# Two stacked blocks on one core: the operands of the split products moved to one address residue in SBUF

## What is computed

```python
for i in range(DEPTH):                       # first block, DEPTH = 2
    h = h + 0.5 * swiglu(rmsnorm(h, ffn1_norm[i]), ffn1_w_gu[i], ffn1_w_down[i])   # 1024 -> 2816 -> 1024
    u = rmsnorm(h, mix_norm[i])
    b_g, c_g, v_c, q_c, kv_c, k_r, g_conv, g_mla = jnp.split(u @ w_in[i], split_pts, axis=-1)
    y_conv = short_conv_branch(b_g, c_g, v_c, conv_w[i], w_conv_out[i])
    y_mla = mla_branch(q_c, kv_c, k_r, ...)  # latent attention, 8 heads
    h = h + (sigmoid(g_conv) * y_conv + sigmoid(g_mla) * y_mla) @ w_o[i]
    h = h + 0.5 * swiglu(rmsnorm(h, ffn2_norm[i]), ffn2_w_gu[i], ffn2_w_down[i])
    h = h + sigmoid(rmsnorm(h, ple_norm[i]) @ w_ple_gate[i]) * (p[i] @ w_ple_proj[i])
...
for i in range(DEPTH):                       # second block
    u = rmsnorm(h, norm_mix_pre[i]) @ w_in[i]
    # sparse attention over the 64 best keys, a 31-tap convolution, pooling
    h = h + rmsnorm(concat(y_attn, y_conv, y_pool) @ w_out[i], norm_mix_post[i])
    m = square(relu(rmsnorm(h, norm_mlp_pre[i]) @ w_up[i])) @ w_down[i]            # 1024 -> 4096 -> 1024
    h = h + rmsnorm(m, norm_mlp_post[i])
    h = h + sigmoid(h @ ple_gate[i]) * (p[i] @ ple_proj[i])
```

## Time and profile before

| | before |
|---|---|
| three runs, median (lowest, highest) | 1911.18 us (1909.38, 1911.8) |
| span of the profiled execution | 1909.4 us |
| TensorE busy | 1871.4 us, 98% |
| VectorE / ScalarE / GpSimd busy | 1343.1 / 998.8 / 133.0 us |
| chain that ended last | TensorE 84%, VectorE 10%, ScalarE 4% |

### The profile page before, as it was taken

How to read it: one execution, slowest core, us unless ns; L and a number is a source line. 1 busy time by engine, 2 the same in 40 slices (tenths; PEclk the granted TensorE clock), 3 DMA queues, 4 the chain that set the end, 5 groups by cost and what they waited for, 6 DMA issues and landing times.

```text
span 1909.4 us, 36805 instructions
## 1 busy us (share of the span) xinstructions
PE 1871.4 (98%) x16004; PEld 1854.5 (97%) x16004; DVE 1343.1 (70%) x1652; ACT 998.8 (52%) x1243; POOL 133.0 (7%) x110
## 2 busy tenths in 40 slices
PE   8999999999999999999999999999999999899999
PEld 8999999999999999999999999998999999899998
DVE  7755787785558655787776556888865589777655
ACT  6443545564437544545565445767534367654443
POOL 1000000000000000000000000264000006600000
PEclk9999999999999999999999999999999999899999
DMA  8655554465555555535545555423566544237651
GB/s 266 207 189 189 165 171 149 159 210 189 188 192 173 204 199 199 186 119 187 179 155 199 199 199 169 155 89 113 180 200 199 183 139 135 72 114 240 199 193 51
DMA packets 246532, 329.56 MB, mean 173 GB/s; under 512 B 6246, under 2 KB 218788, under 8 KB 246372
## 3 DMA queue, kind: packets, MB, share of 16 engines
q1 hardware_dynamic: 246018, 326.79, 51.9%
q0 software_dynamic: 96, 0.26, 0.1%
q10 hardware_dynamic: 258, 0.16, 0.0%
HBM read 326.14 MB, written 1.05 MB: 171 GB/s over the span
## 4 chain that ended last, share of the span: by engine, by line
PE 84%; DVE 10%; ACT 4%; issue 1%; DMA 1%; ACTq 0%; DVEq 0%; SPq 0%
PE work L2061 19%; PE work L2063 19%; PE work L2062 19%; PE acc L2061 9%; PE acc L2063 8%; PE acc L2062 8%; DVE w_lo L1334 3%; ACT w_hi L795 2%; DVE ra L1347 1%; DVE fa L1784 1%; PE work L2208 1%; DMA raw<-in_w_in_dram 1%; PE acc L2130 1%; DVE fa L1860 0%; DVE fa L1386 0%
## 5 line engine op out<-in xcount | busy, mean ns | idle before, releaser
L1334 DVE TENSOR_TENSOR w_lo<-raw,w_hi 128x2048 fp32r<-128x2048 f32 (+2 forms) x313 | 697.4, 2229 | 109.9 <-ACT w_hi L795 108.0
L2061 PE MATMUL work<-x_rows,w_hi 128*128 128x256 f32 x2560 | 712.3, 278 | 8.0 <-DVE w_lo L1334 4.9
L2062 PE MATMUL work<-x_rows,w_hi 128*128 128x256 f32 x2560 | 707.9, 277 | 0.0
L2063 PE MATMUL work<-x_rows,w_lo 128*128 128x256 f32 x2560 | 707.7, 276 | 0.0
L795 ACT ACTIVATE w_hi<-raw 128x2048 fp32r<-128x2048 f32 (+2 forms) x313 | 578.4, 1854 | 150.6 <-PE work L2063 67.2
L2061 PEld LDWEIGHTS work<-x_rows,w_hi 128*128 128x128 f32 x2560 | 483.8, 189 | 11.3 <-issue 6.2
L2062 PEld LDWEIGHTS work<-x_rows,w_hi 128*128 128x128 f32 x2560 | 483.8, 189 | 0.3
L2063 PEld LDWEIGHTS work<-x_rows,w_lo 128*128 128x128 f32 x2560 | 483.8, 189 | 0.0
L2061 PE MATMUL acc<-ra,w_hi 128*128 128x256 f32 x1352 | 372.4, 275 | 0.0
L2063 PE MATMUL acc<-ra,w_lo 128*128 128x256 f32 x1352 | 372.0, 275 | 0.0
L2062 PE MATMUL acc<-ra,w_hi 128*128 128x256 f32 x1352 | 372.0, 275 | 0.0
(11 more groups left out here) (318 smaller groups left out, 2267.9 us busy)
## 6 DMA issues: line engine op xcount, KB each, us to landing
raw<-in_ffn_w_gu_dram SPq DMA_DIRECT2D x88, 1024.0 KB, 5.1
raw<-in_w_in_dram SPq DMA_DIRECT2D x52, 1024.0 KB, 5.4
raw<-in_ffn_w_down_dram SPq DMA_DIRECT2D x44, 1024.0 KB, 5.0
raw<-in_w_up_dram SPq DMA_DIRECT2D x32, 1024.0 KB, 5.4
raw<-in_w_down_dram SPq DMA_DIRECT2D x32, 1024.0 KB, 4.9
raw<-in_w_mla_out_dram SPq DMA_DIRECT2D x8, 1024.0 KB, 5.5
raw<-in_w_o_dram SPq DMA_DIRECT2D x8, 1024.0 KB, 5.0
raw<-in_w_ple_gate_dram SPq DMA_DIRECT2D x8, 1024.0 KB, 5.0
```

The costliest lines, as they stand in the source:

```text
L1334: v.tensor_tensor(w_lo[:, s, 0:n], raw[:, r, 0:n], w_hi[:, s, 0:n].bitcast(F32), ALU.subtract).then_inc(lo_done.sem, 1)
L2061: pe.matmul(dst, ah, bh, start=start and i == 0, stop=False, skip_group_check=not group)
L2062: pe.matmul(dst, ah, bl, start=False, stop=False, skip_group_check=not group)
L2063: last = pe.matmul(dst, al, bh, start=False, stop=stop and i == len(pairs) - 1, skip_group_check=not group)
```

## The change

The tensors in float32r get a common helper and a common start. `rounded(name, n)` reserves 4 elements (16 bytes) more than asked and returns the tensor behind them. `w_hi` and `w_lo` become the two halves of one tensor `w`. `ra` is made longer, and `ka` and `kb` (now one tensor `keys`, the two interleaved row by row), `vp`, `rot_r` and `zero_r` become parts of it behind the old arena. `x_rows` starts its rows 4 elements in instead of 28. The other tensors are put in another order, and 64 bytes (`apart`) are left between `cols` and `x_rows`. The two memsets of `ka` and `kb` become one of `keys`.

The addresses in the built programs, bytes in a partition, and what they leave modulo 256:

| tile | before | modulo 256 | after | modulo 256 |
|---|---|---|---|---|
| `raw` | 1152 | 128 | 1152 | 128 |
| `w_hi` | 25728 | 128 | 32240 | 240 |
| `w_lo` | 58496 | 128 | 65008 | 240 |
| `xh` (in `x_rows`) | 99568 | 240 | 190192 | 240 |
| `ra` | 188144 | 240 | 128752 | 240 |
| `ka`, `kb` | 137856, 144000 | 128 | in `ra` | 240 |
| `vp` | 150144 | 128 | in `ra` | 240 |
| `rot_r`, `zero_r` | 122144, 123168 | 32 | in `ra` | 240 |
| `fa` | 157312 | 128 | 97920 | 128 |
| `h` | 91264 | 128 | 206592 | 0 |
| `consts` | 115968 | 0 | 26048 | 192 |

No instruction of TensorE or SyncE is added, removed or moved. On ScalarE and VectorE four instructions each write `ka` or `kb` in two pieces instead of one. GpSimd has one memset less.

```diff
-X_SIZE, X_ROW, X_AT = 4124, 256, (28, 2076)
+X_ROW, X_AT = 256, (0, 2048)
...
-RA_AT = 4
+R_AT = 4
+RA_SIZE = 10240
+KEYS = 2 * 3 * 2 * T
+VALUES = 2 * TB * 2 * 192
...
+        def rounded(name, n):
+
+            return sb(name, [P, R_AT + n], F32R)[:, R_AT:R_AT + n]
+
         raw = sb("raw", [P, RAWS, CH])
-        w_hi = sb("w_hi", [P, RING, CH], F32R)
-        w_lo = sb("w_lo", [P, RING, CH], F32R)
+        small = sb("small", [P, 80])
+        consts = sb("consts", [P, C_KEPT])
+        w = rounded("w", 2 * RING * CH).rearrange("p (a s n) -> p a s n", a=2, s=RING)
+        w_hi, w_lo = w[:, 0, :, :], w[:, 1, :, :]
+        joint = sb("joint", [P, 28])
+        fa = sb("fa", [P, 7704])
+        rounded_rows = rounded("ra", RA_SIZE + KEYS + VALUES + 3 * P)
+        ra, at = rounded_rows[:, 0:RA_SIZE], RA_SIZE
+        keys = rounded_rows[:, at:at + KEYS].rearrange("p (a t o n) -> p a t o n", a=2, t=3, o=2)
+        ka, kb = (keys[:, :, :, i, :] for i in range(2))
+        at += KEYS
+        vp = rounded_rows[:, at:at + VALUES].rearrange("p (a t g n) -> p a t g n", a=2, t=TB, g=2)
+        at += VALUES
+        rot_r = rounded_rows[:, at:at + 2 * P].rearrange("p (a n) -> p a n", a=2)
+        zero_r = rounded_rows[:, at + 2 * P:at + 3 * P]
+        cols = sb("cols", [P, 100])
+        sb("apart", [P, 16])
+        x_rows = rounded("x_rows", 2 * KD * T)
         h = sb("h", [P, KD, T])
-        x_rows = sb("x_rows", [P, X_SIZE], F32R)
...
-            gp.memset(ka[:, :, :, :].bitcast(F32), 0.0)
-            gp.memset(kb[:, :, :, :].bitcast(F32), 0.0)
+            gp.memset(keys.bitcast(F32), 0.0)
```

More of the change, by code:

```diff
@@ L310, in semaphore @@
             return ctx.enter_context(nc.semaphore(name))
+        def rounded(name, n):
+            return sb(name, [P, R_AT + n], F32R)[:, R_AT:R_AT + n]
         raw = sb("raw", [P, RAWS, CH])
-        w_hi = sb("w_hi", [P, RING, CH], F32R)
-        w_lo = sb("w_lo", [P, RING, CH], F32R)
+        small = sb("small", [P, 80])
[16 more added lines that the diff above has]
+        x_rows = rounded("x_rows", 2 * KD * T)
         h = sb("h", [P, KD, T])
-        x_rows = sb("x_rows", [P, X_SIZE], F32R)
-        consts = sb("consts", [P, C_KEPT])
-        rot_r = sb("rot_r", [P, 2, P], F32R)
-        zero_r = sb("zero_r", [P, P], F32R)
         vrow = sb("vrow", [P, 2, P])
@@ L326, in build @@
         rstd = sb("rstd", [P, 2, T])
[L327 to L332, removed]
         pw = sb("pw", [P, 2, P])
-        fa = sb("fa", [P, 7704])
-        ra = sb("ra", [P, RA_AT + 10240], F32R)[:, RA_AT:RA_AT + 10240]
         def cut(arena, at, *dims):
```

## The result

The changed kernel takes **1967.14 us** (median of four runs, 1958.28 to 1969.83); the kernel before, on the same chip, 1911.20 (four runs, 1909.38 to 1911.80). The ratio is 1.0287, 95% interval 1.0272 to 1.0302: slower by 55 us by the ratio, 56 by the medians. The forecast was 1993 with a range of 1904 to 2012. The profiled execution took 1958.28 us, the fastest of the four, with a span of 1956.5: 47.1 us more than the span before.

The account below looks back on a forecast made before the run. TensorE, busy 98%, bounds the kernel through its matmul pace. Dense matmuls at 120.0 instead of 113.3 ns, less deductions, gave 84.6 or 83, taken as +82: 1909.4 + 1.8 + 82 = 1993 us, range 1904 to 2012.

Parts of the forecast that it names:

- The mechanism: Split-product matmuls: reading the moving operand and loading the next stationary one interfere depending on both addresses; 113.3 or about 120 ns.
- Row (a): Attention scores in ra: pace goes from 113.3 to 120 ns when the stationary tile goes to 240; gave the lower end, 118.
- (b): Dummy matmuls ahead of the MLP, rot_r and zero_r both at residue 32: steady 120 ns, taken for the new pair.
- 93.6 - 5: Dense matmuls: 13,968 x (120.0 - 113.3) ns, less 5 us already outside the rhythm; 4 us of waits also came off.
- +82: Whole kernel: the slowdown in us taken from two ways of summing, 84.6 and 83.
- Token-major products: Products with weights moving and activations stationary: from 120.1 to 120 ns, so no change in time.
- The likeliest case: Whole kernel slower through loss of the 113.3 ns rhythm: 1962 to 2012 us, chance 0.72.
- Nothing for the rest: Moved ScalarE and VectorE destinations, chunk split, merged memset and interleaved key tiles: no visible change in time.
- The moving address alone decides: Rival: moving at 240 is fast whatever is stationary; dense keeps 113.3, token-major gains, 1905 us; chance 0.17.
- The layout is no matter: Rival: the 6.7 ns come from operand roles or the order of the three matmuls; 1911 us within 4; chance 0.07.
- Collides more: Rival: the new pair is worse than any seen in a steady run, 126 ns a matmul, 2079 us; chance 0.04.
- the sign that would have spoken against the rhythm: Restarts after attention still running down from 119 to 113.3 ns after some ten matmuls would show the rhythm misunderstood.

Follow-up runs that it names:

- experiment 2: Kernel before with only w_hi and w_lo moved from residue 128 to 240: 1966.70 us, ratio 1.0295.
- 9: Changed kernel with the split weights put back to residue 128, the rest of its layout kept: 1910.32 us, ratio 0.9999 against the kernel before.
- 12: Kernel of experiment 2 with its weights 64 bytes further on, at residue 48: 1908.90 us, ratio 1.0001 against the kernel before.
- experiment 10: Kernel before plus 44 added stretches of 60 matmuls: four residue pairs, seven moving widths, fewer stationary columns; paces timed, no kernel time given.
- 4: Kernel before with x_rows and ra moved from residue 240 to 128, weights staying at 128: 1986.73 us, ratio 1.0394.
- 1: Kernel before plus 64 added stretches of 90 matmuls: moving residues 240, 128, 0, 32 against stationary ones 16 bytes apart; four pairs reach 113.3 ns.
- 7: Kernel before with split weights at residue 192 and activations at 128: 1918.72 us (1911.22 to 1928.23, eight runs), ratio 1.0052.
- 5: Kernel before plus 160 added stretches of 60 matmuls: further residues, and five pairs from eight starts each; no pair under 113.33 ns.
- 3: Kernel before with everything behind raw 32 bytes further on, weights at 160, activations at 16: 1909.73 us, ratio 0.9989.
- 6: Changed kernel with no edit, run again for a second profile: 1963.94 us.
- 11: Kernel of 7, unchanged, run again for a second profile: 1917.12 us.

## Why the prediction was right, and where its size was off

**What bounds the kernel** held as written: TensorE stays at 98% busy and 84% of the chain, and only its pace moved.

**The mechanism** held as far as it says that the pace hangs on both addresses, and this much is now shown, not only read off a few threes of matmuls. The weights' residue alone brings the whole loss (experiment 2), taking it back removes it (9), and another good residue removes it too (12). Row (a), the rhythm lost at the moment when the stationary tile goes to 240, was the right piece of evidence. That the read of the moving operand and the load of the next stationary one get in each other's way was my reading of it; no run shows this, and both forms in which experiment 10 put it failed.

**The step that was mis-sized** is the pace of the new pair, "I take 120.0 for the new pair, from (b)". Row (b) had equal residues at 32, and that pair does run at 120.0, as 128/128 does in a whole kernel (4). What I carried over wrongly was that equal residues are alike wherever they stand. At 240, 16 bytes off a multiple of 32, the pair runs at 118.33 mostly, at 116.67 or 120.0 for some stretches. The lower bound from (a), 118, was nearer, and its sum gave 1968 beside 1967 measured. The term measured 57.9 us where the sum had 93.6 - 5; that is 31 us of difference in the profiled run, which was the fastest, and about 22 at the median, if the 8.9 us by which that lies higher are in this term too. In the profiled run the forecast's +82 missed the measured +47 by 35: 30.7 of pace, 5.4 of pauses (the clock's part in them included) and 2.0 of token-major products, less 2.6 by which I had gone under my own first sum and 0.5 of other matmuls.

**The other terms** were near. The pauses hold 9.4 us less, where I had 4, but 6.7 of that is time at half clock, for which the forecast had no term and which differs between runs of one kernel. TensorE's idle time fell by 3.8 us, about the 4 of the sum; the waits for split weights that I had named are only a part of it, 6.9 us before and 5.4 after. For the 120.0 ns of the forecast, experiment 4 is the test: +79.6 us of span, +75.5 at the median, against +82.

**Token-major products** I had left at nothing; they fell from 120.1 to 117.1 ns, 2.0 us. They got the same pair as the dense ones, and the forecast held them at 120 for the reason that the dense ones were put there.

**The range** of 1904 to 2012 holds no change and a small gain too, so that the result lies in it says little. The likeliest case's own 1962 to 2012 is the stricter test, and 1967 lies near its lower end.

**Nothing for the rest** held: the layout without the weights' move gives a ratio of 0.9999 (9). The memset of the keys is one of 2.7 us now, and the split on VectorE takes what it took, 2303 ns beside 2305:

```profile
L1344 DVE TENSOR_TENSOR w<-raw,w 128x2048 fp32r<-128x2048 f32 x291 | 669.8, 2303 | 111.2 <-ACT w L805 110.9
```

**The rivals.** "The moving address alone decides" falls: moving 240 takes every pace from 113.3 to 120.0 (1), and experiment 2 changed the stationary tile alone. "The layout is no matter" falls by the result. "Collides more" falls too, though it isn't absurd: 128/176 ran at 123.3 in the sweep. The marks that I had set were 836 matmuls in the dense window, durations of 281 to 283 and an unchanged token-major window; there came 847 or 859, 281 to 285, and 45 for 44 in 5 us. The restart behind the attention part runs at 117 ns from its start, with no run-in, so the sign that would have spoken against the rhythm did not show. "A pace between, say 116.7, would mean that the mechanism is right and the size off" is what happened.

**The rule.** Same shape, same clock, and 113.3 to 123.3 ns by residues alone (1). The Trainium skill, "TensorE: Matmul & The Clock Gate", section "Step-by-step: what each phase is for", has loading weights take no read bandwidth from the running matmul; if nothing else made a difference, all of these would be one number by that; the measurement decides against this for these operands, without showing that it is the load which takes bandwidth. What inside the chip stands behind the residues (the memory's own division, or the order in which two readers are served) no run here shows.

## What to carry to other kernels

Where TensorE is busy 98% and each matmul has its own load, count matmuls per 100 us in several stages before and after any change of the memory layout, even one that moves no work: a start address that shifted by 64 or 112 bytes was worth 3 to 4% of this kernel. Don't align moving and stationary operands on purpose or read the pace of a pair off another pair; time the pair itself, at its own width, from several starts, and prefer one that settles in one pace, since with a pair that has two the kernel's time went from 1911 to 1928 us between runs (7). And after a change elsewhere in the layout, look first whether the residues of the busiest pair still are what they were.

## What the runs showed of the hardware that was not expected

- For 128 stationary and 256 moving columns in this format the steady pace is mostly one of a few values: 113.33, 116.67, 118.33 and 120.0 ns, with 115.6, 117.8 and 118.7 beside them, and up to 123.3. Nothing came under 113.33 in 228 stretches.
- The pace hangs on both residues, and not on their distance alone; moving operands at 240 gave another table than those at multiples of 32 (1, 5). Shifting the pair 240/128 by 32 changed nothing (113.62 and 113.63 ns, and 120.09 in both kernels, 3).
- One pair can have several paces; a stretch takes one at its start and keeps it for 1,500 matmuls (6, 11). The runs scatter more with 128/192, 17.0 us over eight, than with 240/128, 7.1 over nineteen and 8.0 over thirteen. With 240/240 it is 11.6 and 6.9 over four runs each, where 128/128 and 0/128, which showed one pace, have 8.0 and 6.6 over four.
- At 320 and 384 columns residues cost 2.2 ns at most, at 512 they cost up to 6.7 with another order, at 192 nothing (10). With 64 columns at full clock the steady interval is the one of 192, between 111 and 112 ns.
- While TensorE ran matmuls of 64 columns, one upon another with a load each, the granted clock fell from 1.00 to 0.50; it stayed at 0.50 through those of 128 and rose to 1.00 again during those of 192, in all four rounds (10). What makes it fall was not looked into.
